# Two-by-two block products with seven multiplications for nineteen slabs of the 1024-wide projections, their sums on VectorE

## The chip, the cores and the metric

One core of a Trainium2 chip runs the whole program. The metric is the device time of one execution in microseconds, as the median of several runs. Beside it stands one profiled execution, from which all durations below are read. In its rows PE is TensorE's matrix multiply, PEld its weight load, DVE VectorE, ACT ScalarE, POOL GpSimd and SP the queue that issues most transfers.

## What is computed

Two stacks of two layers each work on 256 tokens of width 1024, everything in float32. The first stack has a gated feed-forward, a mixer (a gated delta rule beside a latent attention) and a second feed-forward; the second has a mixer (forgetting and differential attention in layer 0, a chunkwise recurrence in layer 1), a cross attention to 256 memory tokens, and a feed-forward with a short convolution. The change touches the plain projections `h @ w` with 1024 rows in `w`:

```
# first stack, both layers
y_b = mla(...) @ w_branch_b
y = sigmoid(gate_a) * y_a + sigmoid(gate_b) * y_b
x = x + (1.0 + g2) * (y @ w_out)
# second stack
proj = xn @ w_in                                   # layer 0: forgetting and differential attention
x = x + mlstm_out @ mlstm_w_out                    # layer 1
def memory_cross_attention(xn, memn, wq, wkv, wo): # both layers
    q = split_heads(xn @ wq, XATTN_HEADS)
    ...
    return merge_heads(out) @ wo
```

## The kernel before

Activations lie in SBUF as eight tiles of 128 features by 256 tokens (`x`, `h`, `h2`, `qn`, `gates`). Weights come as slabs of 16 tiles of 128x128 (1 MB) through `ring`, which holds five slabs; SP issues the load of slab i once PE has counted slab i-5 as used (`slab_used`). A projection of 1024 by 1024 is four slabs, called jobs 0 to 3 below; each gives two of the eight output tiles. Job 0 to 3 write PSUM banks 0 to 3.

On PE, `linear` (L528) does this: for each of two output tiles eight matmuls over the input tiles, each with 256 tokens as moving columns. It waits for its operands, for the slab's landing (`slab_wait`, L517) and for the bank (`bank_free`). On DVE, `jobs` (L1689) waits until PE has used the slab, hands the bank to its caller, and the caller empties it: `residual` (L1712) adds it to `x`, lets ACT square the new `x`, scales `x` into `h2` (L1726) and adds the squares (L1741, L1744); `cross` (L2431) multiplies the query projection by the root of the norm (L2434); the branch projection's loop (L2545, L2547) multiplies by a gate, adds the other branch, and then calls `ada_sums` (L1885) for two rows of the modulation vectors (L1895); the mixer's input projection in the second stack writes queries and keys (L2572, L2575), and after job 2 `square_memory` (L1672, L1675) squares the memory tokens.

Block products are already there in the feed-forwards. A slab is then seen as a 2x2 block matrix (odd and even input tiles by the two output tiles), the tokens as two halves of 128, and seven products M1 to M7 take the place of eight. `block_products` (L593) issues them on PE: four matmuls of 128 columns for each, 28 in all. M1 and M2 need the raw slab and the raw tokens alone; M6, M5 and M7 need sums of weight blocks and sums of tokens (`token_sums`, L1747), M3 a sum of weight blocks, M4 a sum of tokens. The products go to two PSUM banks, and `add_products` (L1785) with one more subtraction makes the two output tiles of them.

In the convolution's feed-forward, `conv_pairs` (L611) does five of the 22 slabs of a layer so (`CONV_QUICK`: 4, 7, 10, 13, 16), and `sums_ahead` (L2442) on DVE makes each one's four weight sums ahead of that slab:

```
TT(new[:, 0], w[:, 2], w[:, 3], ALU.add)
TT(new[:, 1], w[:, 0], w[:, 2], ALU.subtract)
D()
TT(new[:, 2], new[:, 0], w[:, 0], ALU.subtract)
D()
TT(new[:, 3], w[:, 1], new[:, 2], ALU.subtract).then_inc(conv_sums, 1)
```

`TT` is a DVE operation on two tensors, `D()` a drain of DVE. Every engine runs its instructions in the order of the program; PE's `wait_ge` holds all that stands behind it on PE. Nothing is scheduled by a planner: the order is written by hand.

Of the kernel before, what the change touches and what calls it, by code (L numbers as in the profile page):

```python
# [24 lines left out]
ALU = mybir.AluOpType  # L25
# [3 lines left out]
P = 128  # L29
# [9 lines left out]
CONV_QUICK = (4, 7, 10, 13, 16)  # L39
TPS = 16  # L40
# [116 lines left out]
def build(nc, wstream, astream, crow, xT, memT, pos, par1, par2, pars, const, outT):  # L157
    ctx = ExitStack()
    with ctx:
# [71 lines left out]
        up_tokens = area(20992, 4, 4, P)  # L231

# [112 lines left out]
        conv_sums = sem("conv_sums")  # L345
        freed = {}
# [68 lines left out]
        def weights_of(kind, i, m=0):  # L415

            return LB[:, i % 2, i // 2 % 2 if kind == "fox" else m]

# [94 lines left out]
        def _(pe):  # L513
            cnt = Count()
            at = [0]

# [10 lines left out]

            def linear(nt, kt, rhs, event=None, tps=TPS, burst=False, after={}, hold=None, late=None):  # L528
# [64 lines left out]
            def block_products(slot, new, bank, rhs, sums_ready):  # L593

                for name, (bk, c) in up_banks.items():
                    if name == "M6":
                        sums_ready()
                    for m in range(4):
                        x1, x2, t = rhs(2 * m), rhs(2 * m + 1), up_tokens[:, m]
# [598 lines left out]
            for layer in range(DEPTH):  # L1198
# [14 lines left out]
                linear(8, KD, lambda k: qn[:, k])  # L1213
                linear(8, KD, lambda k: gates[:, 8 + k], late=KD - 2)
# [4 lines left out]
            linear(16, KD, lambda k: h[:, k], event="operands_of_dve", after={1: norm, 9: norm_memory, 13: token_roots})  # L1219
# [42 lines left out]
            linear(8, KD, lambda k: h[:, k], event="operands_of_dve")  # L1262
# [365 lines left out]
        def _(dve):  # L1628
# [156 lines left out]
            def add_products(c, low, middle, high, wait):  # L1785
# [733 lines left out]
            for layer in range(DEPTH):  # L2519
# [23 lines left out]
                for n0, n, b in jobs(8, KD):  # L2543
# [10 lines left out]
                residual(KD, 32, turn=base + SLABS_1 - 37, **unscaled(bare, 2))  # L2554
# [12 lines left out]
            D()  # L2567
# [135 lines left out]
            residual(KD, None, scaled_to=h2, gain=lambda k: L2(1, "xattn", k))  # L2703
# [29 lines left out]
def slabs_of(*parts, tps=TPS):  # L2733
# [7 lines left out]
    return full.transpose(0, 2, 1, 3).reshape(n, P, TPS * P)  # L2741

# [44 lines left out]
def lay_out(i):  # L2787
    w, ada = [], []
    par1, par2 = [], []
    for l in range(DEPTH):  # L2790
# [24 lines left out]
        w.append(slabs_of(weight_tiles(i["w_branch_b"][l])))  # L2815
        w.append(slabs_of(weight_tiles(i["w_out"][l])))
# [9 lines left out]
    for l in range(DEPTH):  # L2826
        if l == 0:
# [3 lines left out]
            w.append(slabs_of(*[weight_tiles(t) for t in (fq, dq, fk, dk, ff)]))  # L2831
# [12 lines left out]
        w.append(halved_slabs(out) if l == 0 else slabs_of(weight_tiles(out)))  # L2844
        w.append(slabs_of(weight_tiles(i["xattn_wq_2"][l])))
        w.append(slabs_of(weight_tiles(i["xattn_wo_2"][l])))
# [65 lines left out]
```

## Time and profile before

| | |
|---|---|
| median of 3 runs | 2669.41 us (2665.01 to 2669.57) |
| the profiled execution | 2666.76 us |
| its span, first to last instruction | 2665.0 us |
| mean granted TensorE clock | 0.997 of full speed |
| busy share of PE, PEld, DVE, ACT, POOL | 98%, 89%, 61%, 19%, 6% |

Each float32 matmul leaves two records on PE, so 32 records of 128x256 are the 16 matmuls of one slab, and 56 records of 128x128 are the 28 of a block-product slab. A row of the timeline gives start, duration, engine, line, operation and how many records were merged into it; a bracket behind it gives the idle time before it and what ended that.

### The profile page before, as it was taken

Reading aid. Unit: us, or ns where it says so; the run is one execution under the profiler, and the core shown is the slowest. Engines: PE = TensorE matmul, PEld = TensorE weight load, DVE = VectorE, ACT = ScalarE, POOL = GpSimd, SP = SyncE. Lnnn points to the kernel's source line nnn. Section 1 sums busy time; section 2 is a strip of 40 time slices with the busy share of each in tenths; the row PEclk is TensorE's granted clock in tenths of the full one; section 3 lists DMA queues with packets and bytes.
Section 4 is the critical chain, followed back from the end, with each engine's and each line's share of the span. In section 5 each row is a group of like instructions: output and inputs, shape, how many; then the busy total and the mean of one; then the engine's idle time right before and its main releaser. Section 6 shows DMA issues by size and latency. Waiting matters only on the chain.

```text
span 2665.0 us, 42910 instructions
## 1 busy us (share of the span) xinstructions
PE 2624.2 (98%) x17876; PEld 2370.5 (89%) x17876; DVE 1615.0 (61%) x3362; ACT 495.0 (19%) x867; POOL 160.8 (6%) x138
## 2 busy tenths in 40 slices
PE   9999999999999999999999999999999999999998
PEld 7899888778999999888878999988889998888998
DVE  4687665655677778665664666444357752324775
ACT  1011343321000100243431100013110011211000
POOL 0000000000430330000000240000000000000000
PEclk9999999999999999999999999999999999999999
DMA  9887431526446556541345444442334444333442
GB/s 380 313 324 268 157 121 54 201 102 237 169 164 237 201 213 227 212 144 65 127 154 193 159 167 167 158 174 96 126 142 158 159 159 170 123 142 112 158 158 95
DMA packets 74450, 458.95 MB, mean 172 GB/s; under 512 B 8308, under 2 KB 9216, under 8 KB 28176
## 3 DMA queue, kind: packets, MB, share of 16 engines
q1 hardware_dynamic: 73120, 449.34, 46.1%
q0 software_dynamic: 1136, 6.86, 0.7%
q8 instruction: 141, 2.31, 0.3%
q14 instruction: 53, 0.43, 0.0%
HBM read 455.08 MB, written 1.09 MB: 171 GB/s over the span
## 4 chain that ended last, share of the span: by engine, by line
PE 92%; DVE 4%; ACT 1%; DVEq 1%; DMA 1%; issue 1%; ACTq 0%
PE psum L550 20%; PE psum L724 14%; PE psum L782 14%; PE psum L631 9%; PE psum L965 8%; PE psum L830 4%; PE psum L1026 2%; PE psum L607 2%; PE psum L737 2%; PE psum L666 2%; PE psum L653 2%; PE psum L985 2%; PE psum L911 1%; PE psum L842 1%; PE psum L938 1%; DVE aring L1895 1%
## 5 line engine op out<-in xcount | busy, mean ns | idle before, releaser
L550 PE MATMUL psum<-h,ring 128*128 128x256 f32 x1536 | 334.8, 379 | 1.4 <-DVE arena L1869 0.8
L550 PEld LDWEIGHTS psum<-h,ring 128*128 128x128 f32 x1536 | 291.3, 190 | 42.4 <-DVE arena L1869 1.1
L782 PE MATMUL psum<-arena 128*128 128x128 f32 x2112 | 251.3, 276 | 1.9 <-DVE arena L1769 1.9
L782 PEld LDWEIGHTS psum<-arena 128*128 128x128 f32 x2112 | 244.2, 193 | 2.1 <-DVE arena L1769 2.1
L631 PE MATMUL psum<-aring,ring 128*128 128x256 f32 x1088 | 237.3, 379 | 1.7 <-issue 1.7
L965 PE MATMUL psum<-h,ring 128*128 128x256 f32 x1024 | 235.0, 382 | 0.0
L631 PEld LDWEIGHTS psum<-aring,ring 128*128 128x128 f32 x1088 | 205.8, 190 | 29.9 <-issue 2.4
L965 PEld LDWEIGHTS psum<-h,ring 128*128 128x128 f32 x1024 | 190.2, 190 | 28.9 <-issue 3.6
L782 PE MATMUL psum<-arena,ring 128*128 128x128 f32 x1584 | 191.6, 275 | 0.0
L782 PEld LDWEIGHTS psum<-arena,ring 128*128 128x128 f32 x1584 | 184.3, 192 | 0.2
L724 PE MATMUL psum<-arena 128*128 128x128 f32 x1440 | 170.6, 275 | 0.0
L724 PEld LDWEIGHTS psum<-arena 128*128 128x128 f32 x1440 | 165.6, 192 | 0.0
L550 PE MATMUL psum<-arena,ring 128*128 128x256 f32 x720 | 157.1, 380 | 2.9 <-DVE arena L2391 1.9
L1895 DVE SCALAR_TENSOR_TENSOR aring<-aring,condb 128x1024 f32<-128x1024 f32 x128 | 153.2, 1221 | 9.9 <-DMA aring<-astream 8.9
L550 PEld LDWEIGHTS psum<-arena,ring 128*128 128x128 f32 x720 | 136.5, 190 | 22.5 <-DVE arena L2391 2.7
L1282 ACT ACTIVATE sq<-x 128x512 f32<-128x512 f32 x48 | 30.3, 631 | 592.7 <-DVEq L1872 384.5
L724 PE MATMUL psum<-h,ring 128*128 128x128 f32 x960 | 117.0, 275 | 0.0
L479 POOL TENSOR_TENSOR arena<-ring 128x512 f32<-128x512 f32 x60 | 77.4, 1291 | 641.4 <-PE psum L586 422.7
L724 PEld LDWEIGHTS psum<-h,ring 128*128 128x128 f32 x960 | 112.2, 192 | 0.2
L666 PE MATMUL psum<-h,ring 128*128 128x256 f32 x448 | 96.9, 379 | 0.3 <-DVE arena L1955 0.3
L666 PEld LDWEIGHTS psum<-h,ring 128*128 128x128 f32 x448 | 85.0, 190 | 12.2 <-issue 0.6
L1766 DVE TENSOR_TENSOR arena<-ring 128x512 f32<-128x512 f32 x66 | 45.6, 691 | 76.6 <-PE psum L782 75.7
(464 smaller groups left out, 3811.3 us busy)
## 6 DMA issues: line engine op xcount, KB each, us to landing
ring<-wstream SPq DMA_DIRECT2D x349, 1024.0 KB, 4.8
aring<-astream SPq DMA_DIRECT2D x128, 512.0 KB, 4.8
arena<-astream SPq DMA_DIRECT2D x16, 512.0 KB, 18.3
arena<-wstream SPq DMA_DIRECT2D x3, 1024.0 KB, 20.2
arena<-decays POOLq DMA_DIRECT2D x2, 1024.0 KB, 5.0
sq<-decays POOLq DMA_DIRECT2D x2, 1024.0 KB, 5.0
kst<-const SPq DMA_DIRECT2D x1, 1280.5 KB, 9.0
x<-xT SPq DMA_DIRECT2D x1, 1024.0 KB, 4.7
```

Source lines behind the costliest of these rows:

```text
L479: nc.gpsimd.tensor_tensor(new[:, 0], w[:, 2], w[:, 3], ALU.add)
L550: mm = pe.matmul(out, lhsT=tile_at(at[0] % RING, t), rhs=rhs(k), start=k == 0, stop=k == kt - 1)
L607: mm = pe.matmul(psum[:, bank + bk, c * P:(c + 1) * P], lhsT=w, rhs=v, start=m == 0 and name in ("M1", "M5"), stop=m == 3, skip_group_chec ...
L631: mm = pe.matmul(psum[:, s % 4, n * T:(n + 1) * T], lhsT=tile_at(slot, 8 * n + 4 * (k % 2) + k // 2), rhs=rhs(k), start=k == 0, stop=k == ...
L653: mm = pe.matmul(psum[:, s, n * T:(n + 1) * T], lhsT=slab[:, t * P:(t + 1) * P], rhs=h[:, k], start=k == 0 and n == 0, stop=k == KD - 1, s ...
L666: mm = pe.matmul(psum[:, s % 4, n * T:(n + 1) * T], lhsT=tile_at(at[0] % RING, n * KD + k), rhs=h[:, k], start=k == 0, stop=k == KD - 1)
L724: mm = pe.matmul(out, lhsT=w, rhs=v, start=m == 0 and name in ("M1", "M5"), stop=m == 3, skip_group_check=True)
L737: mm = pe.matmul(psum[:, (j + 1) % 4, t * T:(t + 1) * T], lhsT=lhs(k)[:, t * P:(t + 1) * P], rhs=ring[:, at[0] % RING, k * T:(k + 1) * T], ...
L782: mm = pe.matmul(out, lhsT=w, rhs=v, start=m == 0 and name in ("M1", "M5", "M3", "M4"), stop=m == NF // 2 - 1, skip_group_check=True)
L830: mm = pe.matmul(psum[:, memory_bank(kind, job), a * T:(a + 1) * T], lhsT=w, rhs=v, start=k == 0, stop=k == KD - 1)
L965: mm = pe.matmul(psum[:, 6 + job % 2, n * T:(n + 1) * T], lhsT=tile_at(i % RING, f % TPS), rhs=h[:, k], start=k == 0, stop=k == KD - 1)
L1895: STT(out=w, in0=w, scalar=1.0, in1=condb[:], op0=ALU.mult, op1=ALU.mult, accum_out=sums[:, b:b + 1]).then_inc(ada_used, 1)
```

## The change

Three tables name the jobs that become block products: `OUT_QUICK = (1, 2)` for the branch projection of both layers of the first stack, the query and output projections of both cross attentions, and the output projection of the second stack's layer 1 (seven projections, 14 slabs); `LAST_QUICK = (1,)` for `w_out` of both layers (2 slabs); `FOX_QUICK = (1, 3, 5)` for the input projection of the second stack's layer 0 (3 slabs). That is 19 slabs in 10 projections. The host lays the tiles of these slabs out as blocks. The products of a quick slab go to banks 4 and 5, those of job 2 to banks 1 and 2.

On PE, `quick_slab` waits on a new semaphore, `out_summed`, ahead of M6. On DVE, `quick_ahead` stands ahead of each of the ten projections: it makes the token sums of all eight tiles and the weight sums of the first quick slab. The weight sums of each further quick slab stand in `quick_jobs`, behind the emptying of the job just ahead of it. The core of the diff:

```diff
+OUT_QUICK = (1, 2)
+LAST_QUICK = (1,)
+FOX_QUICK = (1, 3, 5)
...
+            def quick_slab(job, rhs, quick):
+
+                slab_wait(at[0])
+                nth = quick.index(job)
+                if nth >= 1 and quick == FOX_QUICK:
+                    pe.wait_ge(bank_free, cnt.value("bank_free", quick[nth - 1] + 1))
+                quick_slabs[0] += 1
+                ready = quick_slabs[0]
+                mm = block_products(at[0] % RING, quick_sums(quick, job), quick_bank(quick, job), rhs,
+                                    lambda: pe.wait_ge(out_summed, ready), out_tokens)
+                mm.then_inc(slab_used, 1)
+                at[0] += 1
...
                 for n in range(nt):
+                    if n // 2 in quick:
+                        if n % 2 == 0:
+                            if job >= 3:
+                                pe.wait_ge(bank_free, cnt.value("bank_free", job - 2))
+                            quick_slab(job, rhs, quick)
+                            left -= TPS
+                            job += 1
+                        if n in after:
+                            after[n]()
+                        continue
...
-                            pe.wait_ge(bank_free, cnt.value("bank_free", s + 1 - n))
+                            pe.wait_ge(bank_free, cnt.value("bank_free", (s if s != 1 else 2) + 1 - n))
...
             def cross(layer):
-                linear(8, KD, lambda k: h2[:, k], event="operands_of_dve", after={1: norm})
+                linear(8, KD, lambda k: h2[:, k], event="operands_of_dve", after={1: norm}, quick=OUT_QUICK)
                 attention("mem")
-                linear(8, KD, lambda k: h[:, k], hold=KD - 2)
+                linear(8, KD, lambda k: h[:, k], hold=KD - 2, quick=OUT_QUICK)
...
+            def out_weight_sums(first, job, quick):
+
+                i = first + job
+                w = ring[:, i % RING].rearrange("p (a t) -> p a t", a=4)
+                new = quick_sums(quick, job).rearrange("p a u t -> p a (u t)")
+                dve.wait_ge(landed[i % RING], landing(i))
+                TT(new[:, 0], w[:, 2], w[:, 3], ALU.add)
+                TT(new[:, 1], w[:, 0], w[:, 2], ALU.subtract)
+                D()
+                TT(new[:, 2], new[:, 0], w[:, 0], ALU.subtract)
+                D()
+                TT(new[:, 3], w[:, 1], new[:, 2], ALU.subtract).then_inc(out_summed, 1)
+
+            def quick_ahead(first, src, quick):
+
+                D()
+                token_sums(src, out_tokens, 0, 4)
+                out_weight_sums(first, quick[0], quick)
+
+            def quick_jobs(first, quick, nt=8):
+
+                turned = fox_quads if quick == FOX_QUICK else out_quads
+                for n0, n, b in jobs(nt, KD):
+                    job = n0 // 2
+                    if job in quick:
+                        at = quick_bank(quick, job)
+                        c = 4 + 4 * (quick.index(job) % 2)
+                        pb = psum[:, at + 1].rearrange("p (a t) -> p a t", a=4)
+                        D()
+                        add_products(c, psum[:, at], pb[:, 0:2], pb[:, 1:3], lambda: None, turned)
+                        TT(turned[:, c + 2], turned[:, 2], psum[:, at, 3 * P:], ALU.subtract)
+                        D()
+                        b = turned[:, c:c + 4].rearrange("p (a u) t -> p a (u t)", a=2)
+                    yield n0, n, b
+                    if job + 1 in quick[1:]:
+                        out_weight_sums(first, job + 1, quick)
...
             def cross(layer):
+                first = DEPTH * SLABS_1 + (layer + 1) * (SLABS_2 // 2) - 41
+                quick_ahead(first, h2, OUT_QUICK)
                 root_of_mean(KD * P)
-                for n0, n, b in jobs(8, KD):
+                for n0, n, b in quick_jobs(first, OUT_QUICK):
                     TT(xq[:, n0:n0 + n], b, both(std[:]), ALU.mult).then_inc(bank_free, 1)
                 memory_attention()
-                residual(KD, None, scaled_to=h2, gain=lambda k: L2(layer, "ffn", k))
+                quick_ahead(first + 4, h, OUT_QUICK)
+                residual(KD, None, scaled_to=h2, gain=lambda k: L2(layer, "ffn", k), steps=quick_jobs(first + 4, OUT_QUICK))
...
+                quick_ahead(base + SLABS_1 - 41, qn, OUT_QUICK)
+                for n0, n, b in quick_jobs(base + SLABS_1 - 41, OUT_QUICK):
                     v = gates[:, 8 + n0:8 + n0 + n]
                     TT(v, v, b, ALU.mult)
                     D()
                     TT(v, v, gates[:, n0:n0 + n], ALU.add).then_inc(bank_free, 1)
                     if n0 < 6:
                         ada_sums(base + SLABS_1 - 40 + n0 // 2)
...
+            quick_ahead(DEPTH * SLABS_1, h, FOX_QUICK)
             root_of_mean(KD * P)
             D().then_inc(operands_of_dve, 1)
-            for n0, n, b in jobs(17, KD):
+            for n0, n, b in quick_jobs(DEPTH * SLABS_1, FOX_QUICK, 17):
```

How the order on the engines changes, at three places. DVE in the query projection of the cross attention, from the norm's root (L1656 to L1650) over the emptying of the four banks (L2434) to the attention's first instruction (L2144); before:

```order
L1650 SCALAR_TENSOR_TENSOR std<-ms,std 128x256
L2434 TENSOR_TENSOR arena<-psum,std 128x512 [waits slab_used] x4
L2144 TENSOR_REDUCE small<-psum 128x2 [waits products_for_dve]
```

and now, where L2518 empties a bank, L1870 to L1773 put seven products together, and L1749 to L1754 are weight sums:

```order
L2518 TENSOR_TENSOR arena<-psum,std 128x512 [waits slab_used]
L1870 COPY arena<-psum 128x128 [waits slab_used]
L1872 TENSOR_TENSOR arena<-arena,psum 128x2x128
L1876 TENSOR_TENSOR arena<-arena,psum 128x256
L1879 TENSOR_TENSOR arena<-arena,psum 128x2x128
L1773 TENSOR_TENSOR arena<-arena,psum 128x128
L2518 TENSOR_TENSOR arena<-arena,std 128x512
L1749 TENSOR_TENSOR arena<-ring 128x512 [waits slab_landed2]
L1750 TENSOR_TENSOR arena<-ring 128x512
L1752 TENSOR_TENSOR arena<-arena,ring 128x512
L1754 TENSOR_TENSOR arena<-ring,arena 128x512
L1870 COPY arena<-psum 128x128 [waits slab_used]
```

The weight sums of job 2 stand behind the emptying of job 1, which itself waits for PE to have used job 1's slab. PE at the output projection of the second stack's layer 1 (operands from `h`, the waits on its first job left out), before:

```order
L550 MATMUL psum<-h,ring 128x256 [waits slab_landed3]
L550 MATMUL psum<-h,ring 128x256 x15
L550 MATMUL psum<-h,ring 128x256 [waits slab_landed4]
L550 MATMUL psum<-h,ring 128x256 x15
L550 MATMUL psum<-h,ring 128x256 [waits slab_landed0,bank_free]
```

and now, jobs 1 and 2 and the first matmul of job 3:

```order
L646 MATMUL psum<-h,ring 128x128 [waits slab_landed3]
L646 MATMUL psum<-h,ring 128x128 x7
L646 MATMUL psum<-arena 128x128 [waits out_summed]
L646 MATMUL psum<-arena 128x128 x11
L646 MATMUL psum<-h,arena 128x128 x4
L646 MATMUL psum<-arena,ring 128x128 x4
L646 MATMUL psum<-h,ring 128x128 [waits slab_landed4]
L646 MATMUL psum<-h,ring 128x128 x7
L646 MATMUL psum<-arena 128x128 [waits out_summed]
...
L589 MATMUL psum<-h,ring 128x256 [waits slab_landed0,bank_free]
```

Eight matmuls (M1 and M2) stand between the start of a quick slab and its wait on `out_summed`; twenty stand behind it. DVE in the input projection of the second stack's layer 0, from the emptying of job 2 on, before:

```order
L2572 TENSOR_TENSOR arena<-psum,std 128x512 [waits slab_used] x3
L1672 TENSOR_TENSOR arena<-arena 128x2048 [waits mem_in]
L1675 TENSOR_TENSOR arena<-arena 128x1024
L1675 TENSOR_TENSOR arena<-arena 128x512
L1675 TENSOR_TENSOR arena<-arena 128x256
L2572 TENSOR_TENSOR arena<-psum,std 128x512 [waits slab_used]
```

and now:

```order
L2660 TENSOR_TENSOR arena<-psum,std 128x512 [waits slab_used]
L1717 TENSOR_TENSOR arena<-arena 128x2048 [waits mem_in]
L1720 TENSOR_TENSOR arena<-arena 128x1024
L1720 TENSOR_TENSOR arena<-arena 128x512
L1720 TENSOR_TENSOR arena<-arena 128x256
L1749 TENSOR_TENSOR arena<-ring 128x512 [waits slab_landed3]
L1750 TENSOR_TENSOR arena<-ring 128x512
L1752 TENSOR_TENSOR arena<-arena,ring 128x512
L1754 TENSOR_TENSOR arena<-ring,arena 128x512
L1870 COPY arena<-psum 128x128 [waits slab_used]
```

The weight sums of job 3 stand behind the squares of the memory tokens.

## Rows read from the trace of the kernel before

**Rows 1.** The page, part 1: busy time, share of the span, instructions.

```profile
PE 2624.2 (98%) x17876; PEld 2370.5 (89%) x17876; DVE 1615.0 (61%) x3362; ACT 495.0 (19%) x867; POOL 160.8 (6%) x138
```

**Rows 2.** The page, part 4: the chain that ended last, by engine.

```profile
PE 92%; DVE 4%; ACT 1%; DVEq 1%; DMA 1%; issue 1%; ACTq 0%
```

**Rows 3.** Who PE waited for: total us, times, longest us; three rows.

```profile
PE psum L681 <- DVE sq L1905: 3.9, 1, 3.9
PE psum L926 <- DVE arena L2118: 3.6, 2, 1.8
...
PE psum L782 <- DVE arena L1769: 1.9, 1, 1.9
```

**Rows 4.** Stretches: length, busy of each engine, granted clock, DMA share, GB/s.

```profile
1893.16:1913.88 20.72, 20.72 (x97) 18.24 (x96) 3.78 (x7) 0.89 (x2) 0.00 (x0) 1.00 0.44 153
1986.71:1992.97 6.26, 6.26 (x58) 6.25 (x57) 5.01 (x12) 0.51 (x1) 0.00 (x0) 1.00 0.47 168
2026.85:2033.10 6.25, 6.25 (x58) 6.25 (x56) 4.56 (x10) 0.51 (x1) 0.00 (x0) 1.00 0.46 168
```

**Rows 5.** Timeline of PE, a block-product slab of `conv_pairs` and its successor.

```profile
1986.71 1.95 PE L607 MATMUL psum<-aring,ring 128*128 128x128 f32 x16
1988.50 2.84 PE L607 MATMUL psum<-arena 128*128 128x128 f32 x24
...
1992.97 13.98 PE L631 MATMUL psum<-aring,ring 128*128 128x256 f32 x64
```

**Rows 6.** Timeline of DVE, first and last of four weight sums in `sums_ahead`.

```profile
2003.31 0.68 DVE L2449 TENSOR_TENSOR arena<-ring 128x512 f32<-128x512 f32 x1
...
2005.43 0.69 DVE L2454 TENSOR_TENSOR arena<-ring,arena 128x512 f32<-128x512 f32 x1
```

**Rows 7.** Timeline of DVE, first of five instructions joining seven products, then the emptying.

```profile
1993.17 0.29 DVE L1788 COPY arena<-psum 128x128 f32<-128x128 f32 x1
...
1995.23 0.69 DVE L2463 TENSOR_TENSOR cbuf<-arena,std 128x512 f32<-128x512 f32 x1
```

**Rows 8.** Timeline of DVE, first of four token sums, then what follows them.

```profile
664.37 0.69 DVE L1751 TENSOR_TENSOR arena<-h 128x512 f32<-128x512 f32 x1
...
667.11 1.50 DVE L1947 SCALAR_TENSOR_TENSOR arena<-arena,small 128x256 f32<-128x256 f32 x1
```

**Rows 9.** Timeline, query projection, layer 0: DVE's last squares, PE's jobs 1 to 3.

```profile
1886.91 0.43 DVE L1738 TENSOR_TENSOR sq<-sq 128x256 f32<-128x256 f32 x1
...
1893.16 20.88 PE L550 MATMUL psum<-aring,ring 128*128 128x256 f32 x96
```

**Rows 10.** Timeline of DVE, output projection, layer 0, job 1: emptying, then the squares.

```profile
1944.05 0.69 DVE L1717 TENSOR_TENSOR x<-x,psum 128x512 f32<-128x512 f32 x1 [5.53 <-PE psum L550]
...
1945.48 0.69 DVE L1741 TENSOR_TENSOR sq<-sq 128x512 f32<-128x512 f32 x1
```

**Rows 11.** Timeline of DVE, branch projection, layer 0, job 1: emptying, end of row sums.

```profile
609.17 0.69 DVE L2545 TENSOR_TENSOR arena<-arena,psum 128x512 f32<-128x512 f32 x1 [3.09 <-PE psum L550]
...
612.83 0.08 DVE L1895 DVE_READ_ACCUMULATOR aring<-aring,condb 128x1 f32 x1
```

**Rows 12.** Timeline, input projection, second stack, layer 0 (DVE, and PE's jobs from 1 on).

```profile
1693.08 1.76 DVE L2566 MEMSET arena<- 128x2048 f32 x1 [0.55 <-issue]
...
1697.79 27.79 PE L550 MATMUL psum<-h,ring 128*128 128x256 f32 x128
...
1711.81 0.69 DVE L2572 TENSOR_TENSOR arena<-psum,std 128x512 f32<-128x512 f32 x1 [6.21 <-PE psum L550]
1712.42 2.28 DVE L1672 TENSOR_TENSOR arena<-arena 128x2048 f32<-128x2048 f32 x1
1714.77 2.49 DVE L1675 TENSOR_TENSOR arena<-arena 128x1024 f32<-128x1024 f32 x3
```

**Rows 13.** Stretches after PE had been idle, columns as in rows 4.

```profile
185.50:188.90 3.40, 3.40 (x18) 3.40 (x18) 3.40 (x7) 0.00 (x0) 0.00 (x0) 0.50 0.66 234
...
11.40:14.80 3.40, 3.40 (x10) 2.68 (x9) 3.10 (x9) 1.07 (x3) 0.00 (x0) 0.50 1.00 414
...
592.40:596.00 3.60, 3.06 (x15) 2.50 (x16) 0.85 (x2) 1.84 (x3) 0.00 (x0) 1.00 0.39 164
```

More of the change, by code:

```diff
@@ L231, in build @@
         up_tokens = area(20992, 4, 4, P)
+        out_quads = area(0, 12, P)
+        out_tokens = area(6144, 4, 4, P)
+        out_sums = area(14336, 2, 4, 4, P)
+        fox_quads = area(16896, 12, P)
+        fox_sums = area(18432, 2, 4, 4, P)
         qkv = area(0, 24, T)
@@ L345, in build @@
         conv_sums = sem("conv_sums")
+        out_summed = sem("out_summed")
         freed = {}
@@ L417, in weights_of, with quick_bank, quick_sums @@
             return LB[:, i % 2, i // 2 % 2 if kind == "fox" else m]
+        def quick_bank(quick, job):
+            return 1 if quick == OUT_QUICK and job == 2 else 4
+        def quick_sums(quick, job):
+            return (fox_sums if quick == FOX_QUICK else out_sums)[:, quick.index(job) % 2]
         def memory_bank(kind, job):
@@ L515, in _ @@
             at = [0]
+            quick_slabs = [0]
             def slab_wait(i):
@@ L526, in fresh, with linear @@
                 pe.wait_ge(bank_free, cnt.value("bank_free"))
-            def linear(nt, kt, rhs, event=None, tps=TPS, burst=False, after={}, hold=None, late=None):
+            def quick_slab(job, rhs, quick):
[9 more added lines that the diff above has]
+                at[0] += 1
+            def linear(nt, kt, rhs, event=None, tps=TPS, burst=False, after={}, hold=None, late=None, quick=()):
                 pe.wait_ge(bank_free, cnt.value("bank_free", 0 if late is None else -1))
@@ L591, in first_slab, with block_products @@
                 at[0] += 1
-            def block_products(slot, new, bank, rhs, sums_ready):
+            def block_products(slot, new, bank, rhs, sums_ready, tokens=up_tokens):
                 for name, (bk, c) in up_banks.items():
@@ L598, in block_products @@
                     for m in range(4):
-                        x1, x2, t = rhs(2 * m), rhs(2 * m + 1), up_tokens[:, m]
+                        x1, x2, t = rhs(2 * m), rhs(2 * m + 1), tokens[:, m]
                         w, v = dict(M1=(tile_at(slot, m), x1[:, 0:P]),
@@ L1212, in _ @@
                 mla(layer, fill)
-                linear(8, KD, lambda k: qn[:, k])
-                linear(8, KD, lambda k: gates[:, 8 + k], late=KD - 2)
+                linear(8, KD, lambda k: qn[:, k], quick=OUT_QUICK)
+                linear(8, KD, lambda k: gates[:, 8 + k], late=KD - 2, quick=LAST_QUICK)
                 quick_pairs(lambda k: h[:, k], "operands_of_act")
@@ L1217, in _, with fox_token_roots @@
             assert at[0] == DEPTH * SLABS_1, at[0]
-            linear(16, KD, lambda k: h[:, k], event="operands_of_dve", after={1: norm, 9: norm_memory, 13: token_roots})
+            def fox_token_roots():
+                pe.wait_ge(bank_free, cnt.value("bank_free", FOX_QUICK[-1] + 1))
+                token_roots()
+            linear(16, KD, lambda k: h[:, k], event="operands_of_dve", after={1: norm, 9: norm_memory, 13: fox_token_roots},
+                   quick=FOX_QUICK)
             gate_products(32)
@@ L1261, in _ @@
             pe.wait_ge(memory_moved, 16)
-            linear(8, KD, lambda k: h[:, k], event="operands_of_dve")
+            linear(8, KD, lambda k: h[:, k], event="operands_of_dve", quick=OUT_QUICK)
             cross(1)
@@ L1783, in before_down, with add_products @@
                     token_sums(hidden, down_tokens, s // 2, 1).then_inc(weights_summed, 1)
-            def add_products(c, low, middle, high, wait):
+            def add_products(c, low, middle, high, wait, quads=quads):
                 u2, u43, m1 = quads[:, 0:1], quads[:, 1:3], quads[:, 3:4]
@@ L2542, in _ @@
                 mla(layer)
-                for n0, n, b in jobs(8, KD):
+                quick_ahead(base + SLABS_1 - 41, qn, OUT_QUICK)
+                for n0, n, b in quick_jobs(base + SLABS_1 - 41, OUT_QUICK):
                     v = gates[:, 8 + n0:8 + n0 + n]
@@ L2553, in _ @@
                     modulation(layer, 2)
-                residual(KD, 32, turn=base + SLABS_1 - 37, **unscaled(bare, 2))
+                quick_ahead(base + SLABS_1 - 37, gates[:, 8:16], LAST_QUICK)
+                residual(KD, 32, turn=base + SLABS_1 - 37, **unscaled(bare, 2),
+                         steps=quick_jobs(base + SLABS_1 - 37, LAST_QUICK))
                 norm(x, KD, lambda k: mulc[:, 16 + k:17 + k], h)
@@ L2702, in _ @@
             cnt.seen["slab_used"] += 8
-            residual(KD, None, scaled_to=h2, gain=lambda k: L2(1, "xattn", k))
+            first = DEPTH * SLABS_1 + SLABS_2 - 45
+            quick_ahead(first, h, OUT_QUICK)
+            residual(KD, None, scaled_to=h2, gain=lambda k: L2(1, "xattn", k), steps=quick_jobs(first, OUT_QUICK))
             cross(1)
@@ L2741, in slabs_of, with block_slabs @@
     return full.transpose(0, 2, 1, 3).reshape(n, P, TPS * P)
+def block_slabs(slabs, quick):
+    for j in quick:
+        slabs[j] = slabs[j].reshape(P, 2, KD // 2, 2, P).swapaxes(2, 3).reshape(P, TPS * P)
+    return slabs
 def pair_slabs(a, b):
@@ L2814, in lay_out @@
         w.append(slabs_of(weight_tiles(i["w_branch_a"][l])))
-        w.append(slabs_of(weight_tiles(i["w_branch_b"][l])))
-        w.append(slabs_of(weight_tiles(i["w_out"][l])))
+        w.append(block_slabs(slabs_of(weight_tiles(i["w_branch_b"][l])), OUT_QUICK))
+        w.append(block_slabs(slabs_of(weight_tiles(i["w_out"][l])), LAST_QUICK))
         w.append(quarter_pair_slabs(i["ffn2_w1"][l], i["ffn2_w3"][l]))
@@ L2830, in lay_out @@
             fq, fk, fv, ff, dq, dk, dv = (win[:, at[n]:at[n + 1]] for n in range(7))
-            w.append(slabs_of(*[weight_tiles(t) for t in (fq, dq, fk, dk, ff)]))
+            w.append(block_slabs(slabs_of(*[weight_tiles(t) for t in (fq, dq, fk, dk, ff)]), FOX_QUICK))
             w.append(token_slabs(np.concatenate([fv, dv], 1)))
@@ L2843, in lay_out @@
         w.append(token_slabs(wkv[:, D:]))
-        w.append(halved_slabs(out) if l == 0 else slabs_of(weight_tiles(out)))
-        w.append(slabs_of(weight_tiles(i["xattn_wq_2"][l])))
-        w.append(slabs_of(weight_tiles(i["xattn_wo_2"][l])))
+        w.append(halved_slabs(out) if l == 0 else block_slabs(slabs_of(weight_tiles(out)), OUT_QUICK))
+        w.append(block_slabs(slabs_of(weight_tiles(i["xattn_wq_2"][l])), OUT_QUICK))
+        w.append(block_slabs(slabs_of(weight_tiles(i["xattn_wo_2"][l])), OUT_QUICK))
         up = np.asarray(i["ffn_w_up_2"][l])
```

1 line of the change is left out of this document (removed).

## The prediction, made before the changed kernel had run

> **What bounds the kernel now.** I read the page's part 1 first: PE is busy for 98% of the span, DVE for 61% [rows 1]. A busy PE need not be a PE at its peak, so the chain that ended last came next: 92% of the span lies on PE and 4% on DVE [rows 2]. Then the list of what PE waited for. Its longest wait is 3.9 us, at the program's start, and the next longest are 1.9 and 1.8 us [rows 3]; none of these three lies in a projection that the change touches, and no transfer is in that list. So the time is the sum of what PE issues, and DVE has some 1050 us to spare over the span. Two rules of reading follow. What PE no longer has to do is gained one for one. And what PE is made to wait for is lost one for one, however idle DVE is on average: the question is only whether DVE's work is done by the moment PE asks for it.
>
> **What a slab of block products saves on PE.** The trace has both forms beside each other. Three plain slabs take 20.72 us, so one takes 6.91 us; two block-product slabs in the convolution's feed-forward take 6.26 and 6.25 us [rows 4]. The clock is at full speed in all three stretches. The saving is 6.91 - 6.255 = 0.65 us a slab, and for 19 slabs 12.4 us. It is less than one part in eight (0.86 us), because 28 matmuls of 128 columns cost slightly more per column than 16 of 256. I take the measured value; the bounds are 0.65 and 0.86 us, 12.4 and 16.4 us in all. The laying out of the blocks is done on the host and costs the chip nothing.
>
> **What DVE gets to do, and when PE asks for it.** Four pieces, each with a row of the same operation and size. Weight sums: four instructions, from 2003.31 to 2005.43 + 0.69, so 2.81 us [rows 6]. Token sums of eight tiles: 667.11 - 664.37 = 2.74 us [rows 8]. Joining seven products: 1995.23 - 1993.17 = 2.06 us until the bank can be emptied [rows 7]. And DVE starts on a finished slab 0.20 us after PE has begun the next one (1993.17 against 1992.97) [rows 5, 7]. Against these stands PE's cover inside a quick slab: M1 and M2 need no sums, and last from 1986.71 to 1988.50, 1.79 us [rows 5]. Then PE waits on `out_summed`, and all that stands behind, the other 20 matmuls of the slab and the whole program, waits with it.
>
> *The first quick slab of a projection (job 1).* PE asks 6.91 + 1.79 = 8.70 us after the start of job 0. DVE needs 2.74 + 2.81 = 5.55 us after its last older instruction. In the query projection it ends that one at 1886.91 + 0.43 = 1887.34, so the sums are there at 1892.89, and PE asks at 1893.16 + 1.79 = 1894.95 [rows 9]: hidden, with 2.1 us to spare. The other projections with eight output tiles have the same form: DVE's last write of an operand lies near the start of job 0, and it may lie 3.1 us behind it before PE waits. The nearest to that is `w_out` of layer 1, where two small modulation steps stand ahead of the sums; I put it at zero, with 1 us as its bound. One place fails: in the input projection of the second stack DVE first clears `va`, until 1693.08 + 1.76 = 1694.84, so the sums come at 1700.39, while PE asks at 1697.79 + 1.79 = 1699.58 [rows 12]. Cost 0.8 us. The norm's root, which the first sums now precede, moves back there by some 2 us, under cover of job 1; nothing else waits for it.
>
> *The second quick slab (job 2).* Its sums stand behind the emptying of job 1, and that can't begin before PE has finished job 1, which is the moment when PE begins job 2. Nothing is ahead any more. Counted from PE's start of job 2:
>
> - Query projections, two: 0.20 + 2.06 + 0.61 (one emptying instruction until the next starts, 1712.42 - 1711.81 [rows 12]) + 2.81 = 5.68 us. PE asks at 1.79. Stall 3.9 us, twice, 7.8 us.
> - Projections that end in `residual`, three (both cross attentions, layer 1's mixer): behind the emptying stand the scaling into `h2`, ACT's squares and their sum, 1945.48 - 1944.05 = 1.43 us more [rows 10]. Stall 5.3 us, three times, 16.0 us.
> - Branch projections, two: emptying and the two row sums take 612.83 + 0.08 - 609.17 = 3.74 us [rows 11] in place of 0.61. Stall 5.68 - 0.61 + 3.74 - 1.79 = 7.0 us, twice, 14.0 us.
> - Input projection, job 3: job 2 is plain there, so no joining, but the squares of the memory stand ahead, 1714.77 + 2.49 - 1711.81 = 5.45 us [rows 12]. Stall 0.20 + 5.45 + 2.81 - 1.79 = 6.7 us. Job 5: 0.20 + 0.61 + 2.81 - 1.79 = 1.8 us.
>
> `w_out` has only one quick slab and no second stall. Together 0.8 + 7.8 + 16.0 + 14.0 + 6.7 + 1.8 = 47.1 us, about one tenth of it uncertain either way, since drains and semaphores move single steps by some tenths of a us.
>
> The same machinery in the convolution's feed-forward doesn't stall, and its rows say why: the sums there end at 2006.12 [rows 6], ahead of the slab, with at least two plain slabs between quick ones for DVE to work in. The changed projections put two quick slabs side by side.
>
> *What else moves.* Joining and emptying a quick slab ends 0.20 + 2.06 + 0.7 = 3 us into a following slab of 6.9 us, with the row sums about 6 us in; so the last bank is emptied as before and no projection ends later for it. The new bank wait ahead of the memory attention (job 2's emptying) is met the same way. DVE is busy for some 2.8 us more in each of ten projections and 4.6 us for each of 19 slabs, 115 us, nearly all of it in its idle time. SP issues the same transfers; slabs are counted as used later only where PE itself is later.
>
> **The clock.** After the wait of 1.9 us before L782, the granted clock is 0.50 from 185.50 to 188.90; after the 3.9 us at the start it is 0.50 from 11.40 to 14.80; after a wait of 1.8 us it stays at 1.00 [rows 3, 13]. 0.50 is the lower of the two levels, 1.2 against 2.4 GHz. Each fall costs half of 3.4 us, so 1.7 us of PE's work. Eight of the new stalls last 3.9 us or more (2 + 3 + 2 + 1), as long as the longest or longer: 8 x 1.7 = 13.6 us. For the stalls of 1.8 and 0.8 us I take nothing; the 1.8 us wait in the trace had no fall. Bounds for a stall: no fall at all, and 3.4 us lost where the lower clock lasts twice as long as seen.
>
> The rule that speaks against this change is in the Trainium skill, "TensorE: Matmul & The Clock Gate", section "HAM oscillation — how this bites in real kernels": a loop that alternates short bursts of matmuls with waits pays the return to the lower clock again and again. By that rule the change costs more than its waits; a sum without it would end 13.6 us lower, at 2704 us. The two rows at 0.50 agree with it.
>
> **The sum.** 47.1 + 13.6 - 12.4 = 48.3 us. The profiled execution took 2666.76 us against a median of 2669.41, so it stands for the others within 0.1%; on it the sum gives 2715.1 us, on the median 2717.7. I predict 2718 us, 1.8% slower. About 0.2%, some 5 us, is what a measurement of this kernel can tell from no change.
>
> **Rivals.**
>
> *A: stalls, but the clock stays at its upper level.* For it: one wait of 1.8 us without a fall. Against it: both longer waits had one. Then 2669.4 + 47.1 - 12.4 = 2704 us.
>
> *B: each fall costs 3.4 us.* The lower clock could begin inside the stall, last into the slab, and not be given back by a burst of 4.5 us. The rows show 3.4 us at 0.50 each time, against it. 2669.4 + 47.1 + 27.2 - 12.4 = 2731 us.
>
> *C: the stalls aren't there, faster.* If DVE had job 2's sums before PE asks, only the saving is left: 2669.4 - 12.4 = 2657 us. The mechanism would be that the sums get done inside job 1, where DVE idles for some 3 us even in the branch projection [rows 11]. DVE would have to run job 2's weight sums before it waits for job 1's slab. Its order of instructions says the reverse, and it runs them in that order. It decides at an emptying-to-sums chain of under 1.79 us; the weight sums alone are 2.81.
>
> *D: the change lands within 0.2%.* The stalls would have to add up to 12 us in place of 47, some 1.2 us for each place. Each second slab has at least 2.81 + 0.20 - 1.79 = 1.2 us, so this is the floor that would hold if joining and emptying cost nothing. The rows of the same instructions say 2.7 us for these.
>
> **How the numbers follow.** The forecast: 0.68, with its own range from 47.1 less a tenth and half the clock's cost (2707) to a tenth more and half again (2729). A: 0.12. B: 0.10. C: 0.04. D: 0.02. Something still slower than B, by waits that I have not seen: 0.04. The range takes in the forecast, A and the lower part of B: 2701 to 2733. Faster is C, 0.04; same is D with a little of C and A's neighbours, 0.03; slower is the rest, 0.93.
>
> **What would show each step.** The list of what PE waited for should have a new entry on the line of `block_products`, released by DVE's fourth weight sum, with about ten waits, the longest near 7 us, 47 us in all. The timeline should show 16 records, a gap, then 40, in each second quick slab, and none at first quick slabs save one. A quick slab without a stall should last 6.25 us. The granted clock should show 0.50 some eight times after the gaps, for 3.4 us each. DVE's busy time should rise to 1730 us. I am wrong in the main step if the weight sums of job 2 end before M2, and wrong in the size if the clock holds or if stalls are covered by something that I took to be behind them.

## The result, and the profile after

The changed kernel takes 2717.9 us in the median (2716.29 to 2721.68, 4 runs) against 2667.49 us before (4 runs). The ratio is 1.0191 with a 95% interval from 1.0174 to 1.0209: 1.9% slower. The profiled execution has a span of 2714.5 us against 2665.0.

Busy time on the page of the changed kernel, part 1, beside rows 1:

```profile
PE 2629.3 (97%) x18332; PEld 2389.7 (88%) x18332; DVE 1722.6 (63%) x3573; ACT 495.2 (18%) x867; POOL 160.4 (6%) x138
```

DVE has 107.6 us more than before. PE has 5.1 us more, though it issues fewer columns. The list of what PE waited for, beside rows 3 (total us, times, longest us):

```profile
PE psum L646 <- DVE arena L1754: 46.2, 10, 6.9
PE psum L720 <- DVE sq L1987: 4.3, 1, 4.3
PE psum L965 <- DVE arena L2200: 3.6, 2, 1.8
...
PE psum L821 <- DVE arena L1851: 0.4, 1, 0.4
```

The first row is new: L646 is the matmul of `block_products`, L1754 the last of the four weight sums. Its 46.2 us are close to the loss of 49.5 us in the span, but they aren't the whole account: the saving and the clock stand beside them, as shown below. The next two are those of before. The last is a wait that lasted 1.9 us in the trace before [rows 3], with a fall of the clock behind it [rows 13]; it lasted 0.4 us here and had no fall behind it (the clock is at 1.00 from 179 to 200 us), which by itself makes this trace some 3 us shorter.

The timeline of PE in the branch projection of layer 0, both quick slabs and the start of job 3:

```profile
599.17 1.95 PE L646 MATMUL psum<-arena,ring 128*128 128x128 f32 x16
600.95 3.74 PE L646 MATMUL psum<-arena 128*128 128x128 f32 x32
604.52 2.84 PE L646 MATMUL psum<-arena,ring 128*128 128x128 f32 x24
614.27 5.98 PE L646 MATMUL psum<-arena 128*128 128x128 f32 x32 [6.91 <-DVE arena L1754]
620.09 1.06 PE L646 MATMUL psum<-arena,ring 128*128 128x128 f32 x8
620.99 13.98 PE L589 MATMUL psum<-arena,ring 128*128 128x256 f32 x64
```

The first quick slab runs through: its sums were there. The third row holds the end of it (M4) and M1 and M2 of the second; then PE is idle for 6.91 us. The fourth row is the second thing to see: 32 records took 5.98 us where the same 32 took 3.74 two rows above. The clock had fallen. DVE in the same stretch:

```profile
605.68 0.29 DVE L1870 COPY arena<-psum 128x128 f32<-128x128 f32 x1 [2.58 <-PE psum L646]
...
607.73 0.69 DVE L2631 TENSOR_TENSOR arena<-arena 128x512 f32<-128x512 f32 x1
608.50 0.69 DVE L2633 TENSOR_TENSOR arena<-arena 128x512 f32<-128x512 f32 x1
609.11 1.22 DVE L1977 SCALAR_TENSOR_TENSOR aring<-aring,condb 128x1024 f32<-128x1024 f32 x1
...
611.40 0.68 DVE L1749 TENSOR_TENSOR arena<-ring 128x512 f32<-128x512 f32 x1
...
613.52 0.69 DVE L1754 TENSOR_TENSOR arena<-ring,arena 128x512 f32<-128x512 f32 x1
```

Joining, gating, two row sums, and only then the weight sums. The bracket on the first row says that DVE had been idle for 2.58 us before it. That is time for most of these sums, which take 2.81 us.

Four of the stretches behind a wait (length, busy of PE, PEld, DVE, ACT, POOL, granted clock, DMA share, GB/s). Each begins with the matmul that had waited and ends with the slab:

```profile
614.27:620.99 6.72, 6.72 (x41) 6.72 (x42) 0.00 (x0) 0.00 (x0) 0.00 (x0) 0.66 0.11 43
1925.36:1931.56 6.20, 6.20 (x41) 6.20 (x42) 0.00 (x0) 0.00 (x0) 0.00 (x0) 0.72 0.01 3
1748.34:1752.91 4.57, 4.57 (x41) 4.57 (x41) 0.00 (x0) 0.00 (x0) 0.00 (x0) 1.00 0.16 63
...
2469.67:2477.08 7.41, 7.41 (x41) 7.41 (x41) 0.00 (x0) 0.00 (x0) 0.00 (x0) 0.60 0.01 2
```

At full speed these 40 records take 4.47 us, from 1988.50 to 1992.97 [rows 5]. The waits of 0.8 us and of 1.3 us (the third row here) leave the clock at 1.00. All eight longer ones are followed by a lower mean clock, and their stretches last 6.72, 6.73, 6.16, 6.20, 7.28, 6.56, 6.19 and 7.41 us; together with 0.1 us at each of the two short waits that is 17.7 us over full speed. So the account is 46.2 + 17.7 - 12.4 (the saving) = 51.5 us; less 3.3 us for the old wait that was nearly absent here, plus 0.4 at the start, 48.6 of the 49.5 us. The last 0.9 us is not assigned.

Where the lower level lies decides what a fall costs. The first stretch here is the wait of 6.91 us up to the fall of the clock, the second is the fall; the third is the fall behind a wait of 3.85 us:

```profile
607.36:611.98 4.62, 0.01 (x1) 0.00 (x0) 4.47 (x9) 0.00 (x0) 0.00 (x0) 1.00 0.63 235
611.98:618.81 6.83, 4.54 (x21) 4.54 (x22) 2.09 (x4) 0.00 (x0) 0.00 (x0) 0.50 0.42 131
1926.11:1929.52 3.41, 3.41 (x18) 3.41 (x17) 0.00 (x0) 0.00 (x0) 0.00 (x0) 0.50 0.02 5
```

In the first case the clock fell at 611.98, while PE still waited, and stayed at 0.50 for 6.83 us. Of these, 4.54 us fell on work, and half of that, 2.27 us, is the loss (2.25 us measured). In the other the clock fell when PE was at work again, for 3.41 us. Both waits of the query projections (3.85 us) are of the second kind. The other six are of the first: 0.50 for 6.8 us each, of which 0.8 to 3.5 us lay inside the wait. Half of the part on work gives each of the eight losses within 0.1 us.

### The profile page after: what moved, and what is told of

Same layout as the page of the kernel before. It is cut to its first block, busy times and chain, and to the rows that moved or that the text cites. A ratio compares the mean times of both kernels' runs of the same rounds, so it can differ in the third digit from the quotient of the medians.

```text
span 2714.5 us, 44194 instructions
## 1 busy us (share of the span) xinstructions
PE 2629.3 (97%) x18332; PEld 2389.7 (88%) x18332; DVE 1722.6 (63%) x3573; ACT 495.2 (18%) x867; POOL 160.4 (6%) x138
## 4 chain that ended last, share of the span: by engine, by line
PE 91%; DVE 5%; DVEq 1%; DMA 1%; ACT 1%; issue 1%; ACTq 0%
PE psum L589 15%; PE psum L763 14%; PE psum L821 14%; PE psum L670 9%; PE psum L1004 8%; PE psum L646 7%; PE psum L869 4%; PE psum L1065 2%; PE psum L705 2%; PE psum L776 2%; PE psum L692 2%; PE psum L1024 2%; PE psum L950 1%; PE psum L881 1%; PE psum L977 1%; DVE aring L1977 1%
## 5 line engine op out<-in xcount | busy, mean ns | idle before, releaser
L589 PE MATMUL psum<-h,ring 128*128 128x256 f32 x1248 | 273.3, 379 | 1.4 <-DVE arena L1951 0.8
L589 PEld LDWEIGHTS psum<-h,ring 128*128 128x128 f32 x1248 | 236.1, 190 | 34.7 <-DVE arena L1951 1.1
L821 PE MATMUL psum<-arena 128*128 128x128 f32 x2112 | 249.7, 275 | 0.4 <-DVE arena L1851 0.4
L821 PEld LDWEIGHTS psum<-arena 128*128 128x128 f32 x2112 | 242.6, 192 | 0.6 <-DVE arena L1851 0.6
L1004 PE MATMUL psum<-h,ring 128*128 128x256 f32 x1024 | 235.0, 382 | 0.0
L1004 PEld LDWEIGHTS psum<-h,ring 128*128 128x128 f32 x1024 | 190.2, 190 | 28.9 <-issue 3.6
L821 PEld LDWEIGHTS psum<-arena,ring 128*128 128x128 f32 x1584 | 184.3, 192 | 0.2
L763 PE MATMUL psum<-arena 128*128 128x128 f32 x1440 | 170.6, 275 | 0.0
L763 PEld LDWEIGHTS psum<-arena 128*128 128x128 f32 x1440 | 165.6, 192 | 0.0
L646 PE MATMUL psum<-arena 128*128 128x128 f32 x744 | 105.1, 307 | 46.2 <-DVE arena L1754 46.2
L646 PEld LDWEIGHTS psum<-arena 128*128 128x128 f32 x744 | 101.3, 221 | 48.1 <-DVE arena L1754 48.1
L1870 DVE COPY arena<-psum 128x128 f32<-128x128 f32 x113 | 33.0, 292 | 165.0 <-PE psum L646 98.3
L589 PE MATMUL psum<-arena,ring 128*128 128x256 f32 x528 | 116.3, 380 | 2.9 <-DVE arena L2473 1.9
L589 PEld LDWEIGHTS psum<-arena,ring 128*128 128x128 f32 x528 | 99.7, 190 | 17.3 <-DVE arena L2473 2.7
L763 PEld LDWEIGHTS psum<-h,ring 128*128 128x128 f32 x960 | 112.2, 192 | 0.2
```

Of the source, the lines that this page charges most:

```text
L646: mm = pe.matmul(psum[:, bank + bk, c * P:(c + 1) * P], lhsT=w, rhs=v, start=m == 0 and name in ("M1", "M5"), stop=m == 3, skip_group_chec ...
L763: mm = pe.matmul(out, lhsT=w, rhs=v, start=m == 0 and name in ("M1", "M5"), stop=m == 3, skip_group_check=True)
L821: mm = pe.matmul(out, lhsT=w, rhs=v, start=m == 0 and name in ("M1", "M5", "M3", "M4"), stop=m == NF // 2 - 1, skip_group_check=True)
L1004: mm = pe.matmul(psum[:, 6 + job % 2, n * T:(n + 1) * T], lhsT=tile_at(i % RING, f % TPS), rhs=h[:, k], start=k == 0, stop=k == KD - 1)
```

## The experiments

Each is an edit of the changed kernel. The times of the kernel before, with which each is compared, were taken on the same chip as the experiment.

### Weight sums two jobs ahead

```diff
                     yield n0, n, b
-                    if job + 1 in quick[1:]:
-                        out_weight_sums(first, job + 1, quick)
+                    if job + 2 in quick[1:]:
+                        out_weight_sums(first, job + 2, quick)
```

> The weight sums of a quick slab stand behind the emptying of the job two ahead of it in place of the job just ahead (job 0 for job 2; jobs 1 and 3 for jobs 3 and 5 of the input projection). Nothing else changes. My theory (47 us of stalls and their clock falls stand for the whole loss): of the ten waits on the weight sums only the one of 0.8 us at the input projection is left, no granted clock of 0.50 in the changed projections, and the time is 2667.5 - 12.4 + 0.8 = 2656 us, 0.4% under the kernel before. Rival (DVE's 108 us of additional work or the second set of operands slows PE or the other engines as well): the stalls go, but the time stays above 2664 us.

Measured: 2653.45 us against 2665.91 before, ratio 0.9953 (0.994 to 0.9965), 12.5 us faster (9 to 16 us by the interval). In its list of waits the sums have one row left, and the longest entry is the old one at the start:

```profile
PE psum L720 <- DVE sq L1987: 3.7, 1, 3.7
...
PE psum L646 <- DVE arena L1754: 0.8, 1, 0.8
```

The timeline shows DVE doing job 2's sums in the query projection of layer 0 in the time in which it had been idle:

```profile
1891.17 0.69 DVE L2518 TENSOR_TENSOR arena<-psum,std 128x512 f32<-128x512 f32 x1
1891.78 0.68 DVE L1749 TENSOR_TENSOR arena<-ring 128x512 f32<-128x512 f32 x1
...
1893.90 0.69 DVE L1754 TENSOR_TENSOR arena<-ring,arena 128x512 f32<-128x512 f32 x1
1894.98 0.29 DVE L1870 COPY arena<-psum 128x128 f32<-128x128 f32 x1 [0.39 <-PE psum L646]
```

and PE's two quick slabs back to back, with 6.25 us from the first to the second (1888.46 to 1894.71) and 6.26 us to job 3 (1900.97):

```profile
1888.46 1.95 PE L646 MATMUL psum<-aring,ring 128*128 128x128 f32 x16
...
1894.71 1.95 PE L646 MATMUL psum<-aring,ring 128*128 128x128 f32 x16
1896.50 2.84 PE L646 MATMUL psum<-arena 128*128 128x128 f32 x24
...
1900.97 1.25 PE L589 MATMUL psum<-aring,ring 128*128 128x256 f32 x5
```

The rival falls: DVE is as busy as in the changed kernel (1723.5 us), and PE pays nothing for it that the times can show. The whole loss came from where the sums stand. The one wait on the sums that is left is the one expected, at the input projection.

One part of the expectation was missed. There is a stretch at 0.50 that lies mostly in a changed projection, the branch projection of layer 1. It stands behind a wait of 1.81 us that the kernel before has too and that is not on the sums:

```profile
1417.15 0.55 PE L965 MATMUL psum<-kst,arena 128*128 128x128 f32 x3 [1.81 <-DVE arena L2200]
...
1418.46:1425.29 6.83, 6.31 (x16) 4.87 (x17) 5.35 (x9) 1.12 (x1) 0.00 (x0) 0.50 0.01 5
```

It costs this execution, the slowest of the five, some 3 us (half of 6.31). In the trace of the kernel before, the clock held behind the same wait.

### Weight sums ahead of the joining

```diff
                     job = n0 // 2
+                    if job + 1 in quick[1:]:
+                        out_weight_sums(first, job + 1, quick)
                     if job in quick:
...
                     yield n0, n, b
-                    if job + 1 in quick[1:]:
-                        out_weight_sums(first, job + 1, quick)
```

> The weight sums of a quick slab stay behind PE's use of the job just ahead, but ahead of the joining and emptying of that job. My theory: nine waits of 0.20 + 2.81 - 1.79 = 1.2 us and one of 0.8 us, 11.8 us in all; the clock doesn't fall at any of them, since it held at waits of 1.3 and 1.8 us; the time is 2667.5 - 12.4 + 11.8 = 2667 us, level with the kernel before. Rival (short waits next to each other bring the clock down too): some 1.7 to 2.2 us more at each, up to 2685 us. Rival (the wait is set by something else than the order on DVE): it stays near 2718 us.

Measured: 2664.41 us against 2665.91, ratio 0.9995 (0.9985 to 1.0004): level, as expected. The list of waits and one stretch behind such a wait:

```profile
PE psum L646 <- DVE arena L1754: 10.7, 10, 1.2
...
609.51:614.10 4.59, 4.59 (x41) 4.59 (x42) 4.18 (x8) 0.00 (x0) 0.00 (x0) 1.00 0.38 150
```

Ten waits of at most 1.2 us, 10.7 us in all against 11.8 worked out, and the clock at 1.00. It is the same work and the same number of waits as in the changed kernel, only shorter, and the 12.4 us saved just cover them. So the price of a place is the time from PE's end of the job ahead to the end of the sums on DVE, less 1.79 us of cover.

### The stalls filled with matmuls

```diff
+KEEP = {2: 15, 5: 15, 8: 14, 11: 8, 13: 12, 15: 12, 17: 8, 19: 12}
...
+                def sums_ready():
+
+                    for _ in range(KEEP.get(ready, 0)):
+                        pe.matmul(psum[:, 6, 0:T], lhsT=ones, rhs=K("cmask")[:, 0:T], start=True, stop=True)
+                    pe.wait_ge(out_summed, ready)
+
                 mm = block_products(at[0] % RING, quick_sums(quick, job), quick_bank(quick, job), rhs,
-                                    lambda: pe.wait_ge(out_summed, ready), out_tokens)
+                                    sums_ready, out_tokens)
```

> The changed kernel with 8 to 15 matmuls of 128x256 whose result nobody reads, put on PE between M2 and the wait on the sums, in the eight quick slabs with the long waits: 8 (3.5 us) at the query projections, 12 (5.2 us) at the three that end in the residual, 15 (6.5 us) at the branch projections, 14 (6.0 us) at job 3 of the input projection. PE works through the stall in place of idling, and the stall itself is as long as before. My theory: the clock stays at 1.00, the eight slabs' last 20 matmuls take 4.5 us each in place of 6.2 to 7.3, and the time is 2717.9 - 17.7 = 2700 us. Rival (the slower matmuls behind the stalls have another cause than the idle time): the time stays at 2718 us with 0.50 in the granted clock.

Measured: 2702.56 us against 2665.91, ratio 1.0138 (1.0124 to 1.0151). The changed kernel's ratio is 1.0191, so the filling gains 0.0053 of the kernel before, 14 us; the two intervals don't overlap. The list of waits, the same place in the branch projection, and the two stretches (L653 and L1761 are here what L646 and L1754 were, and L556 is a matmul whose result nobody reads):

```profile
PE psum L653 <- DVE arena L1761: 4.8, 10, 1.3
...
608.60 6.64 PE L556 MATMUL psum<-kst 128*128 128x256 f32 x30
615.68 3.84 PE L653 MATMUL psum<-arena 128*128 128x128 f32 x32 [0.44 <-DVE arena L1761]
...
608.60:615.24 6.64, 6.64 (x32) 5.52 (x30) 6.34 (x12) 0.00 (x0) 0.00 (x0) 1.00 0.79 245
615.68:620.25 4.57, 4.57 (x41) 4.57 (x41) 0.00 (x0) 0.00 (x0) 0.00 (x0) 1.00 0.19 75
```

PE gets no further during the stall than before, but it works, and the 32 records behind it take 3.84 us in place of 5.98. The clock is at 1.00 in both stretches. Its fall and its cost hang on the idle time, not on anything in the slab. The spans differ by 15.0 us where 17.7 was expected; this run reached the branch projection's second quick slab 1.4 us later than the changed kernel (615.68 against 614.27 at the same distance from the slab's start), a delay from before any edit of it had acted, and each of the eight restarts still costs 0.1 us (3.84 against 3.74). With these the two agree within 1 us.

### Clearing behind the first sums

The edit of the first experiment, and

```diff
-            V.memset(va, 0.0)
             quick_ahead(DEPTH * SLABS_1, h, FOX_QUICK)
+            V.memset(va, 0.0)
             root_of_mean(KD * P)
```

> As e1_sums_two_ahead, and in the input projection of the second stack the clearing of va stands behind the first sums in place of ahead of them. My theory: the last wait, 0.8 us, goes too, and the time is 2667.5 - 12.4 = 2655 us, 0.8 us under e1, too little to be told apart by the times; the list of waits shows it. Rival: the norm's root moves back with the clearing and makes a new wait at a later job.

Measured: 2653.93 us against 2665.91, ratio 0.9955 (0.9942 to 0.9967), span 2650.6 us. The list of waits has no row for L646 any more: the wait of 0.8 us that the first experiment still had is gone, and no new one has come. The times don't tell the two apart, as expected. The spans of the two traces differ by 3.1 us, more than the wait of 0.8 us: the first experiment's trace had the fall behind the wait of 1.81 us, and this one held at 1.00 there.

### A second quick slab in `w_out`

The edit of the last experiment, and

```diff
-LAST_QUICK = (1,)
+LAST_QUICK = (1, 2)
```

> As e4_two_ahead_memset_later, and LAST_QUICK is (1, 2) in place of (1,), so that w_out of both layers has two quick slabs side by side, the second one's sums made behind the emptying of job 0. Read from e4's trace: DVE works on job 0 until 4.8 us after its end, then 2.8 us on the sums (just in time for PE, 0.3 us to spare), then 6.6 us on job 1 and 7.4 us on job 2, so it is through with job 2 some 2.0 us after PE has finished job 3. My theory (PE's saving counts only while DVE keeps up to the end of the projection): each layer gains 0.65 us and loses 2.0 us at the norm behind w_out, the waits of PE on the lines of the first slab and the norm grow by some 4 us in all, and the span is 2.7 us longer than e4's. Rival (whatever DVE is late with is hidden behind the first slab of the feed-forward): 1.3 us shorter than e4.

Measured: 2653.58 us against 2665.22 on another chip, ratio 0.9957 (0.994 to 0.9974), span 2652.5 us, 1.9 us longer than the last one's (2.7 us longer was expected, 1.3 us shorter by the rival); the times don't tell the two apart, the traces do. In layer 0 PE and DVE show, at the end of `w_out`:

```profile
646.58 2.77 PE L625 MATMUL psum<-arena,ring 128*128 128x257 f32 x12
651.27 1.11 PE L837 MATMUL psum<-sq,kst 128*128 128x256 f32 x2 [1.92 <-DVE sq L1820]
652.18 5.82 PE L625 MATMUL psum<-arena,ring 128*128 128x257 f32 x20
...
648.68 0.87 DVE L1802 SCALAR_TENSOR_TENSOR x<-psum,mulc,x 128x256 f32<-128x256 f32 x2
```

PE ends job 3 at 646.58, 0.65 us earlier than with one quick slab (647.23), but DVE begins to empty it only at 648.68, 2.1 us later. PE then waits 1.92 us at the norm, and the 20 records behind it take 5.82 us, against 4.51 with one quick slab: a fall of the clock that my sum did not have. In layer 1 DVE is not late at the norm; there job 1 takes 6.55 us and job 2 6.83 us in place of 6.25 each, since both sums just miss PE, by 0.2 and 0.3 us, and the layer ends 0.2 us later than with one quick slab. So the mechanism is right for layer 0, and my claim that both layers lose 2 us at the norm is wrong for layer 1. The waits at the norm grew from 2.9 to 4.6 us in the list, 1.7 us in place of some 4 us. The wait on the sums in layer 1 is a row of the list, 0.3 us.

## Why the prediction was right, point by point

*What bounds the kernel.* Right. PE's chain set the time, and both kinds of terms, matmuls taken away and waits put in, came out one for one. One reading of the list was wrong. I called 1.9 and 1.8 us the next longest waits after 3.9 us, but the list of the kernel before also has

```profile
PE psum L798 <- DVE sq L1738: 2.9, 3, 2.6
```

This longer wait, 2.55 us, ends at 2656.11, at the norm behind the last projection, and only 0.70 us of PE's work stands behind it. It is the same in the changed kernel, so the sum isn't touched.

*The saving.* 0.65 us a slab was predicted from slabs of the same form; 6.25 and 6.26 us were measured in the changed places, and the saving, 12.4 us predicted, is seen with nearly all stalls gone in the first experiment, 12.5 us with one wait of 0.8 us left, and with all of them gone when the clearing stands behind the first sums, 12.0 us.

*First quick slabs.* Predicted hidden, save one with 0.8 us. The list has ten waits: the nine second slabs (two of them later slabs of the input projection) and this one, 0.79 us. All other first slabs ran through, `w_out` of layer 1 too.

*Second quick slabs.* Predicted 3.9 us at the query projections, measured 3.85 and 3.85; 5.3 at those that end in `residual`, measured 5.35, 5.40 and 5.35; 7.0 at the branch projections, measured 6.91 twice; 6.7 and 1.8 at the input projection, measured 6.50 and 1.30. In all 47.1 against 46.2 us. The only term off by more than 0.2 us is job 5 of the input projection, 1.30 in place of 1.8: the norm of the memory tokens issues a matmul between jobs 4 and 5, so job 5 begins 0.43 us after job 4's end (1745.09 against 1737.75 + 6.91), and I had left that out.

*The clock.* This is the term that was mis-sized: 1.7 us for each of eight falls, 13.6 us, against 17.5 us measured. The number of falls was right. The 1.7 us was half of 3.4 us, read behind two waits where the clock fell only after PE was at work again. That held for the two shortest of the eight waits (1.72 and 1.73 us lost). Behind the other six the level of 0.50 lasted 6.8 us and began inside the wait, which left 3.4 to 6.0 us of work under it, so these cost 1.69 to 2.94 us each. The range had room for it. The warning that I took from the Trainium skill, "TensorE: Matmul & The Clock Gate", section "HAM oscillation — how this bites in real kernels", is that bursts which alternate with waits pay for the return to the lower clock each time. This trace agrees as far as it goes: each of the eight waits of 3.85 us and more was paid for, and the experiment that fills the stalls takes the payment away. A loop of short bursts, the skill's own case, was not run here: more than 20 us lie between any two of the eight waits.

*The sum.* 48.3 us were predicted and 50.4 measured by the medians. That the predicted time, 2718 us, and the measured one, 2717.9, agree to 0.1 us is luck; the terms don't agree so well. The clock's term was 4 us too small, and against it stands the wait of 1.9 us with its fall that the trace before had and this one had not, and a median of the kernel before that was 1.9 us lower than the one the forecast started from.

*The rivals.* (The lower end of the forecast's own range, given as 2707, comes out of its terms as 2706.) A, a clock that holds, is out by 14 us, the gain from filling the stalls. B, 3.4 us for each fall, is out by the sum, 17.5 against 27.2, but its mechanism is half of what happened: at six of the eight the lower clock did begin inside the stall and last into the slab. It cost less than 3.4 us because the part inside the stall costs nothing. C, hidden stalls, is what the kernel does once the sums stand two jobs ahead; and D's floor of 1.2 us at each place is what the second experiment measured, 1.13 to 1.19 us at eight of the nine places and 0.70 at job 5 of the input projection.

*DVE.* Busy time was predicted at 1730 us and came out at 1722.6.

## What to carry to other kernels

When work on a second engine must be ready for the bounding one, look at what it stands behind in its own order, not at how busy that engine is: here the same instructions at three places in DVE's order gave 50 us lost, no change that the times can show, and 12 us gained. Price a wait from the moment at which the engine waited for is released, add each instruction ahead of the one that is needed, and take off the cover that the waiting engine has. A stall of TensorE of some 4 us or more costs a further 1.7 to 2.9 us here through its clock.

## What the runs showed of the hardware

- In the changed kernel the granted clock held at 1.00 behind the waits of 0.79 and 1.30 us and fell at all eight of 3.85 to 6.91 us. In between it is not settled by length alone: it fell behind waits of 1.95 and 1.92 us, and the same wait of 1.81 us in layer 1 had no fall in the kernel before and one of 6.83 us in the first experiment.
- A fall lasted 3.4 or 6.8 us, and what it cost was half of the part that lay on work, 1.69 to 2.94 us for the same 40 records. The length of the wait doesn't order the costs (6.50 us of waiting cost 1.69, and 5.35 us cost 2.94). The place of the fall does: with 6.50 us, 3.45 of the 6.83 us at 0.50 lay inside the wait, with 5.35 us only 0.84. Why the clock fell where it did is open here.
- The stretch behind the wait of 1.92 us in the last experiment shows the fall setting in only when PE was at work again (0.58 over 0.93 us, then 0.77), so a wait's own row doesn't tell whether it will cost more than its length (columns as in rows 4):

```profile
649.34:651.27 1.93, 0.01 (x1) 0.00 (x0) 1.67 (x5) 0.63 (x1) 0.00 (x0) 1.00 0.83 276
651.27:652.20 0.93, 0.93 (x3) 0.74 (x4) 0.00 (x0) 0.00 (x0) 0.00 (x0) 0.58 0.94 357
652.18:657.84 5.66, 5.66 (x22) 4.72 (x20) 4.59 (x12) 3.26 (x8) 0.00 (x0) 0.77 0.33 125
```
